# A two-layer hybrid attention decoder on one core: first four tiles side by side over pieces of weights and activations

## The chip, the cores and the metric

The kernel runs on one core of a Trainium2 chip. The metric is the device time of one execution in microseconds (us); lower is better. Inputs lie in the chip's memory at the start, the output there at the end.

## The reference, cut to what matters

Two layers on 272 tokens (16 learned ones and 256 of x) with 1024 channels, all in float32:

```
h    = rms_norm(r, norm_mix_pre[layer])
proj = h @ w_in[layer]          # q latent | kv latent | rope key | dq | dk | dv | gate_A | gate_B
out_a = causal_attention(...) @ w_o_mla      # from the latents
out_b = causal_diff_attention(...) @ w_o_diff
mix  = (sigmoid(g_a) * out_a + sigmoid(g_b) * out_b) @ w_out
r    = r + rms_norm(mix, norm_mix_post)
h    = rms_norm(r, norm_ffn_pre)
r    = r + rms_norm((silu(h @ w_gate) * (h @ w_up)) @ w_down, norm_ffn_post)
```

`rms_norm(x, gain)` is x / sqrt(mean(x*x) + 1e-6) * gain. The change touches the first norm of layer 0 and the first six column tiles of its `proj` (the latents and the rope key).

## The kernel before

**Layout.** Activations lie transposed: 128 channels on the partitions, 272 tokens in a row, 8 chunks of channels (`KC`). A tile is 128 columns of a weight matrix for all tokens, in one PSUM bank: 8 chunks k times three matmuls of 128x272. Three, because each float32 operand is split into a rounded part (`hi`, type fp32r) and a rest (`lo`): hi x hi, lo x hi and hi x lo are summed.

**Weights.** They are packed on the host into slots of 128 x 1024 values (512 KB), one for a tile of `proj`. SP (the sync engine) loads slot n into `w_raw[n % 4]`, and has to wait until VectorE has taken slot n - 4 apart (`lo_ready`, L285). ScalarE (ACT) rounds a slot into `w_hi` (`split`, L334 to L344), VectorE (DVE) subtracts into `w_lo` (`split`, L693 to L701); `w_hi` and `w_lo` are rings of 8.

**The norm.** The factor 1/sqrt(mean) belongs to a token, so it is applied when a tile is evacuated (`evac`, L715), not to the activations before. ScalarE multiplies the residual by the gain and rounds it (`first_hi`, L380), VectorE makes the rest (`lo_part`, L720). ScalarE also squares the residual (`square`, L346); GpSimd (POOL) adds up the squares of chunks 0 to 6 (`sum_squares`, L619), with two buffers for squares, so that a square waits for the add two before. TensorE (PE) sums over the partitions with 12 matmuls against ones (`norm_sums`, L1163), ScalarE takes the root (`root`), VectorE the reciprocal (`recip`), TensorE spreads it over the partitions by three transposes (`norm_spread`, L1194) and VectorE copies it out as `rstd_h` (`take`, L710). Only then can tile 0 be evacuated.

**Banks.** Tiles go round four banks (`t % BANKS`); a tile waits until the one four before it has been evacuated (`bank_free`, L1102). Bank 7 holds the norm's sums and its spread, bank 6 the throwaway matmuls of `keep_clock` (L1182).

**The order at the start.** SP issues, in this order: gains, x chunks 0-1, the first half of slots 0 and 1 together, x 2-3, x 4-5, the second half, x 6-7, the identity, slots 2, 3, 4, the rotary tables, slot 5, masks and lambdas (L291 to L305). ScalarE and VectorE work on slots 0 and 1 in quarters (`quarter_split`, L385 and L750). TensorE runs 50 throwaway matmuls (L1199), then tiles 0 and 1 side by side, chunk after chunk (`first_tiles`, L1123), tile 2, the norm's sums, tile 3 with the spread before its chunk 6, and tiles 4 and 5 (L1222). VectorE's order behind the spread: for each of the five latent tiles an evacuation, a weight split and a `lat_lo` (L810 to L822), with masks and lambda sums after the fourth; then the rotary factors, a split and tile 5 (L827 to L838); then the tiles of dq, dk and so on.

Of the kernel before, what the change touches and what calls it, by code (L numbers as in the profile page):

```python
# [23 lines left out]
P = 128  # L24
# [72 lines left out]

C_ID, C_MASK, C_MASKM, C_COSD, C_SIND, C_COSM, C_SINM = 0, 128, 256, 512, 784, 1056, 1328
# [49 lines left out]
def build_trunk(nc: bass.Bass, xT, weights, gains, lam_in, consts, gain_rows, out):  # L148
# [4 lines left out]
    with ctx:  # L153
# [3 lines left out]
        def place(at, tensors):  # L157
# [7 lines left out]
        (w_raw, w_hi, w_lo, r, hh, hl, y, rstd_h, rstd_q, acc, sq, rc_d, rs_d, rc_q, rs_q,  # L165
         cst, identb, maskb, gain, small, lat, tres), at = place(base, [
            ("w_raw", [P, RAW, SLOT], f32), ("w_hi", [P, RING, SLOT], f32r), ("w_lo", [P, RING, SLOT], f32r),
            ("resid", [P, KC, TOK], f32), ("h_hi", [P, KC, TOK], f32r), ("h_lo", [P, KC, TOK], f32r),
# [5 lines left out]
            ("gain", [P, DEPTH, GAINS], f32), ("small", [P, 96], f32), ("lat", [P, 2, TOK], f32),  # L174
            ("tres", [P, TOK], f32)])
        lat_tmp_at = at - 4 * 3 * TOK
        rstd_kv = tres
# [6 lines left out]
        k_t = nc.alloc_sbuf_tensor_at("k_t", [P, MLA_HEADS, TOK], f32, offset=base + 4 * (RAW + 2 * RING) * SLOT + 3 * 4 * KC * TOK)  # L184
# [15 lines left out]
        krope = dv_t[:, 0, :]  # L200
        dqk_at = att0 + 4 * MLA_HEADS * TOK
# [7 lines left out]
        (o_tok, o_sq), _ = place(base + 4 * (RAW + 2 * RING) * SLOT + 4 * KC * TOK, [("o_tok", [P, 2, D_MODEL], f32), ("o_sq", [P, 2, D_MODEL], f32)])  # L209
        assert _ <= base + 4 * (RAW + 2 * RING) * SLOT + 12 * KC * TOK  # L210
# [57 lines left out]

        def T0(l):

            return 0 if l < DEPTH - 1 else N_META
# [61 lines left out]
        def _(act):  # L333
            def split(n, i=None, per=0):  # L334
# [5 lines left out]
                act.wait_ge(raw_in[n % RAW], 16 * (n // RAW + (n % RAW >= 2)) + v)  # L340
# [34 lines left out]

            act.wait_ge(const_ready, 1)
            act.activation(idle_act, eps, ACT.Sqrt)
            act.wait_ge(gain_in, 16)

            def first_hi(*chunks):  # L380
                for c in chunks:
                    act.wait_ge(x_in[c // 2], 16)
                    act.activation(hh[:, c, :], r[:, c, :], ACT.Copy, scale=gain[:, 0, G_MIXPRE + c:G_MIXPRE + c + 1]).then_inc(h_hi, 1)

            def quarter_split(q):  # L385
# [21 lines left out]
            for n in range(3, AHEAD):  # L407
                split(n)
# [1182 lines left out]
```

## Time and profile before

| | |
|---|---|
| median of 3 runs | 835.7 us (835.64 to 836.18) |
| the profiled execution | 835.84 us, of which span 834.0 us |
| TensorE busy | 819.4 us (98%) |
| VectorE busy | 595.4 us (71%) |
| ScalarE busy | 451.9 us (54%) |
| GpSimd busy | 123.4 us (15%) |
| read from memory | 129.70 MB |

How to read it: the span is the time from the first to the last instruction, and the shares are of it. A share is a mean over stages with different limits, so the timeline of an engine and the table by stretches of time are read beside it. TensorE's matmuls are pipelined: the time from the start of one to the start of the next is its price, and is shorter than its own duration. The weight load that goes with each matmul overlaps the one before. The granted clock (PEclk) is 1.00 for 2.4 GHz and 0.50 for 1.2 GHz.

### The profile page before, as it was taken

The page shows a single profiled execution, that of the slowest core. Times are in us where ns is not written, and L with a number is a line of the kernel's source. Part 1 is how long each engine was busy: PE and PEld are TensorE (multiplying, and loading weights), DVE is VectorE, ACT ScalarE, POOL GpSimd, SP SyncE. Part 2 cuts the span into 40 slices and gives each one's busy share as a digit, 9 for nine tenths or more (in the row PEclk, how much of TensorE's full clock was granted, in tenths as well). Part 3 has the DMA queues.
Part 4 walks back from the last instruction along what each step waited for, and adds up shares of the span by engine and source line. Part 5 has one row for each costly group of instructions (what it writes and reads, how often), then busy time and mean ns, then how long its engine had stood idle before and what let it go on. Part 6 is the DMA issues. An engine that isn't in the chain of part 4 may idle for free.

```text
span 834.0 us, 17173 instructions
## 1 busy us (share of the span) xinstructions
PE 819.4 (98%) x6453; PEld 792.6 (95%) x6453; DVE 595.4 (71%) x1000; ACT 451.9 (54%) x749; POOL 123.4 (15%) x125
## 2 busy tenths in 40 slices
PE   8999999999999999999999999999999999999997
PEld 8998999999999999999999999899999999999885
DVE  4999586669597666666668995876787976766432
ACT  6755555475565444455556546554765654554431
POOL 2122000004331111101112220000053111111000
PEclk9999999999999999999999999999999999999999
DMA  8656422235526545445552555222363565565631
GB/s 280 224 189 205 148 77 102 76 103 181 173 88 217 180 172 177 131 139 185 178 199 86 200 195 185 95 101 99 108 224 103 182 219 182 177 194 172 207 104 50
DMA packets 38744, 131.55 MB, mean 158 GB/s; under 512 B 4384, under 2 KB 4768, under 8 KB 38688
## 3 DMA queue, kind: packets, MB, share of 16 engines
q1 hardware_dynamic: 38688, 130.77, 47.0%
q8 instruction: 39, 0.64, 0.3%
q14 instruction: 17, 0.14, 0.1%
HBM read 129.70 MB, written 1.05 MB: 157 GB/s over the span
## 4 chain that ended last, share of the span: by engine, by line
PE 84%; DVE 12%; issue 2%; ACT 1%; DMA 1%; SPq 0%; DVEq 0%; POOL 0%; POOLq 0%
PE bank L1110 21%; PE bank L1112 20%; PE bank L1111 20%; DVE w_lo L700 3%; PE bank L1140 3%; PE bank L1462 2%; PE bank L1463 2%; PE bank L1461 2%; PE bank L1335 2%; PE bank L1311 2%; PE bank L1159 2%; PE bank L1144 1%; DVE h_lo L722 1%; PE bank L1350 1%; DVE resid L737 1%
## 5 line engine op out<-in xcount | busy, mean ns | idle before, releaser
L700 DVE TENSOR_TENSOR w_lo<-w_raw,w_hi 128x1024 fp32r<-128x1024 f32 x250 | 336.0, 1346 | 39.2 <-ACT w_hi L344 37.1
L1110 PE MATMUL bank<-h_hi,w_hi 128*128 128x272 f32 (+1 forms) x1232 | 357.6, 290 | 2.1 <-DVE dv_t L718 0.9
L1112 PE MATMUL bank<-h_hi,w_lo 128*128 128x272 f32 (+1 forms) x1232 | 352.1, 286 | 0.0
L1111 PE MATMUL bank<-h_lo,w_hi 128*128 128x272 f32 (+1 forms) x1232 | 351.3, 285 | 0.0
L344 ACT ACTIVATE w_hi<-w_raw 128x1024 fp32r<-128x1024 f32 x250 | 262.6, 1054 | 127.7 <-PE bank L1112 54.7
L1110 PEld LDWEIGHTS bank<-h_hi,w_hi 128*128 128x128 f32 x1232 | 232.0, 188 | 4.2 <-issue 1.3
L1112 PEld LDWEIGHTS bank<-h_hi,w_lo 128*128 128x128 f32 x1232 | 231.9, 188 | 0.0
L1111 PEld LDWEIGHTS bank<-h_lo,w_hi 128*128 128x128 f32 x1232 | 231.6, 188 | 0.0
L624 POOL TENSOR_TENSOR acc<-acc,sq 128x272 f32<-128x272 f32 (+1 forms) x48 | 48.5, 1011 | 148.2 <-ACT sq L357 147.6
L669 POOL TENSOR_TENSOR pbuf<-sbuf,ubuf 128x272 f32<-128x272 f32 (+1 forms) x44 | 37.4, 850 | 210.2 <-DVE ubuf L1048 207.2
L1048 DVE TENSOR_TENSOR ubuf<-bank,rstd_h 128x272 f32<-128x272 f32 (+1 forms) x44 | 19.0, 431 | 48.1 <-PE bank L1112 48.0
L1110 PE MATMUL bank<-ff_hi,w_hi 128*128 128x272 f32 x176 | 50.7, 288 | 0.0
L1112 PE MATMUL bank<-ff_hi,w_lo 128*128 128x272 f32 x176 | 50.6, 288 | 0.0
L1111 PE MATMUL bank<-ff_lo,w_hi 128*128 128x272 f32 x176 | 50.6, 287 | 0.0
L573 ACT ACTIVATE sbuf<-gbuf 128x272 f32<-128x272 f32 (+1 forms) x44 | 18.7, 424 | 54.1 <-DVE gbuf L1048 54.1
L657 POOL TENSOR_TENSOR gates<-gates 128x272 f32<-128x272 f32 (+1 forms) x16 | 15.7, 1004 | 208.9 <-DVE gates L718 208.9
L473 ACT ACTIVATE e_t<-bank,small 128x272 f32<-128x272 f32 x64 | 27.0, 431 | 31.0 <-DVE small L912 31.0
L1140 PE MATMUL bank<-h_hi,w_hi 128*128 128x272 f32 (+1 forms) x144 | 38.6, 295 | 2.2 <-DVE w_lo L754 1.8
L1140 PE MATMUL bank<-h_hi,w_lo 128*128 128x272 f32 (+1 forms) x144 | 37.9, 289 | 0.0
L1462 PE MATMUL bank<-w_lo,ff_hi 128*128 128x512 f32 x88 | 34.7, 395 | 0.0
L1463 PE MATMUL bank<-w_hi,ff_lo 128*128 128x512 f32 x88 | 34.7, 394 | 0.0
L1461 PE MATMUL bank<-w_hi,ff_hi 128*128 128x512 f32 x88 | 34.6, 394 | 0.0
(209 smaller groups left out, 1250.6 us busy)
## 6 DMA issues: line engine op xcount, KB each, us to landing
w_raw<-weights SPq DMA_DIRECT2D x220, 512.0 KB, 4.0
w_raw<-weights SPq DMA_DIRECT2D x16, 384.0 KB, 3.0
w_raw<-weights SPq DMA_DIRECT2D x16, 320.0 KB, 2.8
resid<-x_t SPq DMA_DIRECT2D x4, 272.0 KB, 5.4
out_tokens<-o_tok SPq DMA_DIRECT2D x4, 256.0 KB, 2.0
cst<-consts SPq DMA_DIRECT2D x1, 544.0 KB, 4.9
gain_bc<-gain_rows SPq DMA_DIRECT2D x1, 512.0 KB, 6.7
y<-consts SPq DMA_DIRECT2D x1, 256.0 KB, 5.3
```

The source lines that it names most:

```text
L344: act.activation(w_hi[:, n % RING, :], w_raw[:, n % RAW, :], ACT.Copy).then_inc(hi_ready, 1)
L473: last = act.activation(e_t[:, e, a:b], ps[bank][:, a:b], ACT.Exp, bias=mx[u % 2][:, s + part:s + part + 1], scale=scale, accum_out=sm[u % ...
L624: pool.tensor_tensor(acc[:, K % 2, t0:], acc[:, K % 2, t0:], sq[:, plan.sq_place[K, c], t0:], ALU.add).then_inc(sq_added, 1)
L669: pool.tensor_tensor(pbuf[:, j % 2, t0:], sbuf_[:, j % 2, t0:], ubuf[:, j % 2, t0:], ALU.mult).then_inc(ff_prod, 1)
L700: dve.tensor_tensor(w_lo[:, n % RING, :], w_raw[:, n % RAW, :], w_hi[:, n % RING, :].bitcast(f32), ALU.subtract).then_inc(lo_ready, 1)
L1110: pe.matmul(dst, wh, hi, start=first, stop=False)
L1111: pe.matmul(dst, wh, lo, start=False, stop=False)
L1112: return pe.matmul(dst, wl, hi, start=False, stop=last)
L1140: pe.matmul(ps[t % BANKS][:, t0:TOK], w[:, n % RING, k * P:(k + 1) * P], src[k][0], start=k == 0 and q == 0, stop=False)
L1461: pe.matmul(dst, x_hi, wh, start=k == 0, stop=False)
L1462: pe.matmul(dst, x_hi, wl, start=False, stop=False)
L1463: return pe.matmul(dst, x_lo, wh, start=False, stop=k == FC - 1)
```

## The change

- The first four weight slots come in a tensor of their own, `first_weights`, packed by five pieces of chunks: (0), (1), (2, 3), (4, 5), (6, 7), each with those chunks' columns of all four tiles. They land in a buffer of their own, `w_first`, that lies where later q and k are kept. Gains and x come in one tensor: 80 columns of gains, then x.
- SP issues the five weight pieces, and the x of the last two pieces ahead of their weights. ScalarE issues the x of the first three pieces from its own queue, before anything else.
- Slots 4 to 7 go into the four raw buffers without a wait.
- ScalarE does, for each piece: its activations, their squares, and the split of the piece for four tiles. VectorE does the lo parts and the split of the same piece.
- TensorE runs tiles 0 to 3 side by side, piece by piece: hi x hi of the piece's chunks, then lo x hi, then hi x lo. Tiles 4 and 5 take banks 4 and 5, so that no tile waits for a bank before tile 6. The norm's sums stand at chunk 0 of tile 4, the spread at its chunk 5.
- 34 throwaway matmuls at the start instead of 50.
- On VectorE one split moves from the second latent tile to the third, where two now stand.

```diff
+GAIN_COLS = 80
+FIRST = 4
+PIECES = [(0, 1), (1, 2), (2, 4), (4, 6), (6, 8)]
+X_BY_ACT = 3
...
+            ("x_sb", [P, GAIN_COLS + KC * TOK], f32), ("h_hi", [P, KC, TOK], f32r), ("h_lo", [P, KC, TOK], f32r),
+        r = x_sb[:, GAIN_COLS:].rearrange("p (k t) -> p k t", k=KC)
+        gain = x_sb[:, 0:DEPTH * GAINS].rearrange("p (l g) -> p l g", l=DEPTH)
+        (w_first,), _ = place(att0, [("w_first", [P, FIRST * SLOT], f32)])
...
+        def piece_of(w, a, b):
+            return w[:, FIRST * P * a:FIRST * P * b].rearrange("p (s c) -> p s c", s=FIRST)
+        def x_cols(q):
+            a, b = PIECES[q]
+            return slice(GAIN_COLS + a * TOK if q else 0, GAIN_COLS + b * TOK)
+        def bank_of(t):
+            return t if t < FIRST + 2 else t % BANKS
...
-                if n >= RAW:
+                if n >= FIRST + RAW:
...
-            xc = xT.rearrange("p (k t) -> p k t", k=KC)
-            sp.dma_start(gain[:, :, :], gains.rearrange("p (l g) -> p l g", l=DEPTH)).then_inc(gain_in, 16)
-            two = weights[0:2 * P, :].rearrange("(s p) c -> p s c", s=2)
-            for q in range(4):
-                sp.dma_start(r[:, 2 * q:2 * q + 2, :], xc[:, 2 * q:2 * q + 2, :]).then_inc(x_in[q], 16)
-                if q in (0, 2):
-                    at = q * SLOT // 4
-                    sp.dma_start(w_raw[:, 0:2, at:at + SLOT // 2], two[:, :, at:at + SLOT // 2]).then_inc(half_in[q // 2], 16)
+            for q, (a, b) in enumerate(PIECES):
+                ws = slice(FIRST * P * a, FIRST * P * b)
+                if q >= X_BY_ACT:
+                    sp.dma_start(x_sb[:, x_cols(q)], xT[:, x_cols(q)]).then_inc(x_in[q], 16)
+                sp.dma_start(w_first[:, ws], first_weights[:, ws]).then_inc(piece_in[q], 16)
             sp.dma_start(cst[:, 0:P], consts[:, 0:P]).then_inc(id_in, 16)
-            load(2, SLOT)
-            load(3, SLOT)
             load(4, SLOT)
+            load(5, SLOT)
             sp.dma_start(cst[:, P:], consts[:, 512:C_ALL]).then_inc(tables_in, 16)
-            load(5, SLOT)
+            load(6, SLOT)
+            load(7, SLOT)
             sp.dma_start(stage, consts[:, P:512 + P].rearrange("p (a b) -> p a b", a=2)[:, :, 0:256]).then_inc(mask_in, 16)
             sp.dma_start(lam_raw, lam_in).then_inc(mask_in, 16)
-            first = 6
+            first = FIRST + RAW
...
+            for q in range(X_BY_ACT):
+                act.dma_start(x_sb[:, x_cols(q)], xT[:, x_cols(q)]).then_inc(x_in[q], 16)
...
+            def first_hi(q):
+                act.wait_ge(x_in[q], 16)
+                for c in range(*PIECES[q]):
                     act.activation(hh[:, c, :], r[:, c, :], ACT.Copy, scale=gain[:, 0, G_MIXPRE + c:G_MIXPRE + c + 1]).then_inc(h_hi, 1)
+            def piece_split(q):
+                act.wait_ge(piece_in[q], 16)
+                a, b = PIECES[q]
+                ins = act.activation(w_hi[:, 0:FIRST, a * P:b * P], piece_of(w_first, a, b), ACT.Copy)
+                if b == KC:
+                    ins.then_inc(hi_ready, FIRST)
+                else:
+                    ins.then_inc(piece_hi, 1)
-            first_hi(0, 1)
-            quarter_split(0)
-            quarter_split(1)
-            first_hi(2, 3)
-            first_squares(0, 1)
-            first_hi(4, 5)
-            quarter_split(2)
-            quarter_split(3)
-            first_hi(6, 7)
-            first_squares(2)
-            split(2)
-            first_squares(3, 4, 5, 6, 7)
-            for n in range(3, AHEAD):
-                split(n)
+            for q in range(len(PIECES)):
+                first_hi(q)
+                first_squares(*range(*PIECES[q]))
+                piece_split(q)
+            split(FIRST)
+            split(FIRST + 1)
+            split(FIRST + 2)
...
-                if l == 0:
-                    split(AHEAD)
...
-            for c in range(KC):
-                lo_part(0, c, G_MIXPRE, 0, 0)
-                if c in (1, 5):
-                    quarter_split(c // 2)
-                    quarter_split(c // 2 + 1)
-            split(2)
-            split(3)
-            split(4)
-            split(5)
+            dve.wait_ge(x_in[0], 16)
+
+            def piece_split(q):
+
+                a, b = PIECES[q]
+                if b == KC:
+                    dve.wait_ge(hi_ready, FIRST)
+                else:
+                    dve.wait_ge(piece_hi, q + 1)
+                ins = dve.tensor_tensor(w_lo[:, 0:FIRST, a * P:b * P], piece_of(w_first, a, b), w_hi[:, 0:FIRST, a * P:b * P].bitcast(f32), ALU.subtract)
+                if b == KC:
+                    ins.then_inc(lo_ready, FIRST)
+                else:
+                    ins.then_inc(piece_lo, 1)
+
+            for q, (a, b) in enumerate(PIECES):
+                dve.wait_ge(x_in[q], 16)
+                for c in range(a, b):
+                    lo_part(0, c, G_MIXPRE, 0, 0)
+                piece_split(q)
+            split(FIRST)
+            split(FIRST + 1)
...
-                    if i or not l:
-                        split(S("lat") + i + AHEAD)
+                    if l or i != 1:
+                        if l == 0 and i == 2:
+                            split(S("lat") + 1 + AHEAD)
+                        if i or not l:
...
-                if t >= BANKS:
+                if t >= FIRST + 2:
...
+            def start_tiles(src):
+                for q, (a, b) in enumerate(PIECES):
+                    for k in range(a, b):
+                        pe.wait_ge(h_hi, k + 1)
+                        if b == KC:
+                            pe.wait_ge(hi_ready, FIRST)
+                        else:
+                            pe.wait_ge(piece_hi, q + 1)
+                        for t in range(FIRST):
+                            pe.matmul(ps[t][:, :TOK], w_hi[:, t, k * P:(k + 1) * P], src[k][0], start=k == 0, stop=False)
+                    for k in range(a, b):
+                        pe.wait_ge(h_lo, k + 1)
+                        for t in range(FIRST):
+                            pe.matmul(ps[t][:, :TOK], w_hi[:, t, k * P:(k + 1) * P], src[k][1], start=False, stop=False)
+                    if b == KC:
+                        slot_ready(FIRST - 1)
+                    else:
+                        pe.wait_ge(piece_lo, q + 1)
+                    for k in range(a, b):
+                        for t in range(FIRST):
+                            mm = pe.matmul(ps[t][:, :TOK], w_lo[:, t, k * P:(k + 1) * P], src[k][0], start=False, stop=k == KC - 1)
+                            if k == KC - 1:
+                                mm.then_inc(pe_done, 1)
...
-            keep_clock(50)
+            keep_clock(34)
...
-                    first_tiles([(TL("lat") + q, S("lat") + q, late, t0) for q in range(2)], (h_hi, h_lo, 0),
-                                {0: lambda: pe.wait_ge(quarter_lo, 1), 2: lambda: pe.wait_ge(quarter_lo, 2),
-                                 4: lambda: pe.wait_ge(quarter_lo, 3), 6: lambda: slot_ready(1)})
-                    slot_ready(S("lat") + 2)
-                    tile(TL("lat") + 2, S("lat") + 2, 0, P, late, t0)
-                    norm_sums(K0 + PRE_MIX, 7, 0)
-                    pe.wait_ge(id_in, 16)
-                    slot_ready(S("lat") + 3)
-                    tile(TL("lat") + 3, S("lat") + 3, 0, P, full, 0, inside={6: lambda: norm_spread(K0 + PRE_MIX, 7, 0)})
+                    start_tiles(full)
...
-                    tile(TL("lat") + i, S("lat") + i, 0, P if i < 5 else HW, full, 0)
+                    def first_spread():
+                        pe.wait_ge(id_in, 16)
+                        norm_spread(PRE_MIX, 7, 0)
+                    tile(TL("lat") + i, S("lat") + i, 0, P if i < 5 else HW, full, 0,
+                         inside={0: lambda: norm_sums(PRE_MIX, 7, 0), 5: first_spread} if (l, i) == (0, 4) else None)
...
+    x_t = np.concatenate([gains, np.zeros((P, GAIN_COLS - DEPTH * GAINS), np.float32), x_t], axis=1)
...
+    first = packed[0:FIRST * P].reshape(FIRST, P, SLOT)
+    first = np.concatenate([first[:, :, a * P:b * P].transpose(1, 0, 2).reshape(P, -1) for a, b in PIECES], axis=1)
```

## Rows read from the trace of the kernel before

**Rows 1.** The page: busy us; two groups with busy, mean ns | idle.
```profile
PE 819.4 (98%) x6453; PEld 792.6 (95%) x6453; DVE 595.4 (71%) x1000; ACT 451.9 (54%) x749; POOL 123.4 (15%) x125
...
L700 DVE TENSOR_TENSOR w_lo<-w_raw,w_hi 128x1024 fp32r<-128x1024 f32 x250 | 336.0, 1346 | 39.2 <-ACT w_hi L344 37.1
...
L624 POOL TENSOR_TENSOR acc<-acc,sq 128x272 f32<-128x272 f32 (+1 forms) x48 | 48.5, 1011 | 148.2 <-ACT sq L357 147.6
```

**Rows 2.** TensorE's timeline: start, length, operation, count [idle before <-releaser].
```profile
1.06 5.18 PE L1185 MATMUL bank<-identb 128*128 128x128 bf16 x50 [1.06 <-DVE identb L747]
8.08 0.39 PE L1140 MATMUL bank<-h_hi,w_hi 128*128 128x272 f32 x1 [1.84 <-DVE w_lo L754]
...
10.10 0.43 PE L1140 MATMUL bank<-h_hi,w_hi 128*128 128x272 f32 x1
10.33 0.43 PE L1140 MATMUL bank<-h_hi,w_lo 128*128 128x272 f32 x1
...
15.73 0.28 PE L1110 MATMUL bank<-h_hi,w_hi 128*128 128x272 f32 x1
...
18.76 0.72 PE L1159 MATMUL bank<-small,acc 128*128 128x1 f32 x6
...
20.01 0.37 PE L1110 MATMUL bank<-h_hi,w_hi 128*128 128x272 f32 x1
...
22.48 0.54 PE L1178 MATMUL bank<-cst,small 128*128 128x128 f32 x3
...
40.39 0.36 PE L1110 MATMUL bank<-h_hi,w_hi 128*128 128x272 f32 x1 [0.94 <-DVE dv_t L718]
...
78.13 0.39 PE L1110 MATMUL bank<-lat_hi,w_hi 128*128 128x272 f32 x1 [0.55 <-DVE dv_t L718]
```

**Rows 3.** Stretches: length, busy by engine, granted clock, DMA share, GB/s.
```profile
9.20:12.60 3.40, 3.40 (x18) 3.40 (x17) 3.12 (x7) 3.40 (x9) 0.98 (x2) 0.50 0.89 354
```

**Rows 4.** The same view for VectorE alone.
```profile
23.05:81.70 58.65, 57.00 (x101) 1.00 0.61 203
```

**Rows 5.** VectorE's timeline.
```profile
23.06 0.44 DVE L713 COPY rstd_h<-bank 128x272 f32<-128x272 f32 x1 [0.64 <-PE bank L1178]
23.53 0.44 DVE L718 TENSOR_TENSOR lat<-bank,rstd_h 128x272 f32<-128x272 f32 x1
...
25.85 0.50 DVE L821 SCALAR_TENSOR_TENSOR lat_lo<-lat,gain,lat_hi 128x272 fp32r<-128x272 f32 x1 [0.74 <-ACT lat_hi L425]
...
28.62 1.45 DVE L700 TENSOR_TENSOR w_lo<-w_raw,w_hi 128x1024 fp32r<-128x1024 f32 x1
29.99 1.02 DVE L821 SCALAR_TENSOR_TENSOR lat_lo<-lat,gain,lat_hi 128x272 fp32r<-128x272 f32 x1
```

**Rows 6.** ScalarE's timeline.
```profile
0.74 1.28 ACT L377 ACT_TABLE_LOAD   x1 [0.74 <-PEq L1585]
...
8.56 0.41 ACT L357 ACTIVATE acc<-resid 128x272 f32<-128x272 f32 x1
...
9.20 0.92 ACT L383 ACTIVATE h_hi<-resid,gain 128x272 fp32r<-128x272 f32 x2
10.03 1.14 ACT L389 ACTIVATE w_hi<-w_raw 128x512 fp32r<-128x512 f32 x2
11.06 0.92 ACT L383 ACTIVATE h_hi<-resid,gain 128x272 fp32r<-128x272 f32 x2
```

**Rows 7.** SP's timeline; transfers, us to landing; a stretch as in rows 3.
```profile
1.19 0.42 SPq L294 DMA_DIRECT2D resid<-x_t  x1
1.66 0.43 SPq L297 DMA_DIRECT2D w_raw<-weights  x1
...
resid<-x_t SPq DMA_DIRECT2D x1, 272.0 KB, 3.5
w_raw<-weights SPq DMA_DIRECT2D x1, 512.0 KB, 5.0
...
3.00:5.00 2.00, 2.00 (x22) 2.00 (x21) 0.00 (x0) 0.22 (x1) 0.00 (x0) 1.00 0.92 315
```

More of the change, by code:

```diff
@@ L145, in __init__, with build_trunk @@
                     s += CHUNKS[k]
-def build_trunk(nc: bass.Bass, xT, weights, gains, lam_in, consts, gain_rows, out):
+def build_trunk(nc: bass.Bass, xT, first_weights, weights, lam_in, consts, gain_rows, out):
     f32, f32r, bf16 = mybir.dt.float32, mybir.dt.float32r, mybir.dt.bfloat16
@@ L163, in place @@
             return made, at
-        (w_raw, w_hi, w_lo, r, hh, hl, y, rstd_h, rstd_q, acc, sq, rc_d, rs_d, rc_q, rs_q,
-         cst, identb, maskb, gain, small, lat, tres), at = place(base, [
+        (w_raw, w_hi, w_lo, x_sb, hh, hl, y, rstd_h, rstd_q, acc, sq, rc_d, rs_d, rc_q, rs_q,
+         cst, identb, maskb, small, lat, tres), at = place(base, [
             ("w_raw", [P, RAW, SLOT], f32), ("w_hi", [P, RING, SLOT], f32r), ("w_lo", [P, RING, SLOT], f32r),
-            ("resid", [P, KC, TOK], f32), ("h_hi", [P, KC, TOK], f32r), ("h_lo", [P, KC, TOK], f32r),
+            ("x_sb", [P, GAIN_COLS + KC * TOK], f32), ("h_hi", [P, KC, TOK], f32r), ("h_lo", [P, KC, TOK], f32r),
             ("y", [P, KC, TOK], f32),
@@ L173, in build_trunk @@
             ("cst", [P, C_ALL - 512 + 128], f32), ("identb", [P, P], bf16), ("maskb", [P, P], bf16),
-            ("gain", [P, DEPTH, GAINS], f32), ("small", [P, 96], f32), ("lat", [P, 2, TOK], f32),
+            ("small", [P, 96], f32), ("lat", [P, 2, TOK], f32),
             ("tres", [P, TOK], f32)])
         lat_tmp_at = at - 4 * 3 * TOK
+        r = x_sb[:, GAIN_COLS:].rearrange("p (k t) -> p k t", k=KC)
+        gain = x_sb[:, 0:DEPTH * GAINS].rearrange("p (l g) -> p l g", l=DEPTH)
         rstd_kv = tres
@@ L373, in boundary @@
                     square(K, c, r[:, c, t0:], t0)
+            for q in range(X_BY_ACT):
+                act.dma_start(x_sb[:, x_cols(q)], xT[:, x_cols(q)]).then_inc(x_in[q], 16)
             act.wait_ge(const_ready, 1)
             act.activation(idle_act, eps, ACT.Sqrt)
[L378 to L382, printed above, removed]
+            def first_hi(q):
+                act.wait_ge(x_in[q], 16)
+                for c in range(*PIECES[q]):
                     act.activation(hh[:, c, :], r[:, c, :], ACT.Copy, scale=gain[:, 0, G_MIXPRE + c:G_MIXPRE + c + 1]).then_inc(h_hi, 1)
-            def quarter_split(q):
-                act.wait_ge(half_in[q // 2], 16)
-                cols = slice(q * SLOT // 4, (q + 1) * SLOT // 4)
-                act.activation(w_hi[:, 0:2, cols], w_raw[:, 0:2, cols], ACT.Copy).then_inc(hi_ready if q == 3 else quarter_hi, 2 if q == 3 else 1)
+            def piece_split(q):
[6 more added lines that the diff above has]
+                    ins.then_inc(piece_hi, 1)
             def first_squares(*chunks):
@@ L717, in evac @@
                 dve.wait_ge(pe_done, plan.tile_done[t])
-                dve.tensor_tensor(dst, ps[t % BANKS][rows, t0:TOK], factor, ALU.mult).then_inc(tile_free, 1)
+                dve.tensor_tensor(dst, ps[bank_of(t)][rows, t0:TOK], factor, ALU.mult).then_inc(tile_free, 1)
             def lo_part(b, c, g, l, t0):
@@ L1581 @@
     gain_rows = np.broadcast_to(A(norm_ffn_post)[DEPTH - 1][None, :], (P, D_MODEL))
-    arrays = {"x_t": x_t, "weights": packed, "gains": gains, "lam": lam, "consts": constants(), "gain_rows": gain_rows}
+    first = packed[0:FIRST * P].reshape(FIRST, P, SLOT)
+    first = np.concatenate([first[:, :, a * P:b * P].transpose(1, 0, 2).reshape(P, -1) for a, b in PIECES], axis=1)
+    arrays = {"x_t": x_t, "first_weights": first, "weights": packed, "lam": lam, "consts": constants(), "gain_rows": gain_rows}
     arrays = {k: np.ascontiguousarray(v) for k, v in arrays.items()}
```

27 lines of the change are left out of this document (11 added, 16 removed).

## The prediction, made before the changed kernel had run

> **What bounds the kernel now.** First the page's busy shares: TensorE is busy for 98% of the span [rows 1], so a change can only give time where TensorE idles, runs slowly or does more than it must. Next its own timeline [rows 2]. Fifty warm-up matmuls run from 1.06 to 6.24 us; the first real matmul starts at 8.08, after 1.84 us of idle. From there to 78 us there are few gaps: 0.94 us before 40.39 and 0.55 us before 78.13 are the ones shown, both released by a VectorE evacuation. After 78.13 VectorE is no longer what holds TensorE in this layer. The pitch of a matmul is read from two neighbours: tile 2 has 24 of them from 15.73 to 18.76, 0.126 us each, while at 10.10 and 10.33 the pitch is 0.23. The table by stretches says why: from 9.20 to 12.60 the granted clock is 0.50, which is 1.2 GHz, and the pitch at 15.73 is that of 2.4 GHz again; what TensorE did before that fall was its idle time up to 8.08 [rows 2, 3]. The 48 matmuls of tiles 0 and 1 took 7.65 us (8.08 to 15.73) where 0.126 each gives 6.05, so the low clock cost 1.6 us.
>
> The third view decides the case. From 23.05 to 81.70 VectorE is busy 57.00 of 58.65 us [rows 4], and the only idle time that I find behind its start at 23.06 is 0.74 us at 25.85 [rows 5]. That chain starts when rstd_h is copied out (23.06), runs through evacuations, weight splits and rotary factors, and TensorE, with a ring of four banks, waits for it. The waits at 40.39 and 78.13 are for it. So for this stage the end is set by when the evacuation of tile 0 can start (23.53) and by how long VectorE then needs, not by how early TensorE finished its first tiles. I reason with that start, and call it E.
>
> **Part 1, the start.** Before, x piece 0 is issued at 1.19 and lands 3.5 us later, at 4.7; the first weights, issued at 1.66, land at 6.7 [rows 7]. They were 0.84 MB together with the gains. After, piece 0 is 0.18 MB of x with gains on ACT's queue and 0.26 MB of weights on SP's, both issued at about 0.75. Against x piece 0 of before (0.32 MB with the gains) that is 0.12 MB more, 0.4 us at the 315 GB/s of 3 to 5 us, and the issue is 0.44 us earlier: weights at about 4.7, x at about 4.4. ScalarE's issues are three at SP's 0.42 us each; they push its table load, 0.74 to 2.02, to about 2.1 to 3.4 [rows 6, 7]: hidden behind the landing at 4.4. If an issue on ACT took far longer (1 us), the table would end at 5.1 and all below be 0.7 us late.
>
> ScalarE then works in series. From row to row: two activations 0.83, two squares 0.64, a 512-column split half of 1.03 [rows 6]. Per 128 rows of the model that is 0.42 + 0.32 + 0.52 = 1.25 us, against 12 matmuls at 0.126 = 1.5 us on TensorE. First matmul: 4.4 + 0.5 + 0.4 + 0.6 = 5.95 (from 8.08). The split of piece 2 (512 KB, for k = 2, 3) needs pieces 0 to 2, 1.67 MB: the first 0.84 MB landed at 6.66, the rest at 315 to 354 GB/s [rows 3, 7] takes 2.3 to 2.6 us, less 0.44: 8.5 to 8.8, I take 8.6. ScalarE by its own series is there at about 8.5. Split 1.05: k = 2 is ready at 9.7. TensorE has done k = 0, 1 at 5.95 + 3.0 = 8.95, and stalls 0.75. Pieces 3 and 4 are then ready at intervals of 2.5 us against 3.0 of TensorE, so 72 matmuls follow without a gap: 9.7 + 9.05 = 18.75.
>
> The Trainium skill speaks against a gain from the second queue here (DMA: Bandwidth & Descriptors, section "Issuing engines are not separate DMA queues": transfers from either issuer share the same engines, and only issue time is saved). This trace has no transfer from ACT, so it doesn't show it; by the rule the sum stands as written, and if instead the queues were independent the weights of piece 0 would land some 0.4 us sooner, and ScalarE, waiting for x, would still set 5.95.
>
> **Part 2, from there to E.** Before, the twelve norm-sum matmuls (18.76 to 20.01, 1.25 us) ran behind tile 2, and the spread at 22.48 came with six matmuls of tile 3 left. After, they stand at k = 0 of tile 4 and the spread at k = 5: 18.75 + 1.25 + 15 matmuls 1.9 + a handover of 0.1 + the 1.05 us from spread to evacuation (22.48 to 23.53) [rows 2, 5] = 23.05. So of 2.1 us won at the first matmul, 0.75 goes to the stall and 2.65 to the 21 matmuls that now stand ahead of the spread (96 + 15 where 90 were), while the low clock (1.6 us before) is not in this sum: by these differences E would move by 0.1, by the absolute sum by 0.5, since before had some 0.4 us of small gaps ahead of the spread. I take 0.5.
>
> The clock has to be put back in. Warm-up of 34 ends at about 1.06 + 34 x 0.104 = 4.6, idle is 1.35 us instead of 1.84, plus the stall. Nothing shows that this leaves the clock alone: bounds 0 and 1.6 us (the same fall as before). The first 0.75 us of a fall ahead of 9.7 would vanish in the stall. I take 0.3.
>
> **Part 3, behind E.** The VectorE chain from 23.53 to the evacuation of tile 5, which lets TensorE go on at 40.39, is 16.9 us with 0.74 idle [rows 2, 5]. Its instructions stay; one split moves from the second latent tile to the third. The 0.74 (a late raw weight for ScalarE) goes, since slots 4 to 7 are loaded without waiting for a free buffer. In its place the second lat_lo, no longer behind a split, must wait for ScalarE's split, activation and square: about 0.5. 16.9 - 0.74 + 0.5 is 16.6, so -0.3. Bounds: -1.2 (both go, and one of the two lat_lo that took 1.02 instead of 0.50 runs free) and +0.5. TensorE has tiles 4 to 8 done by about 18.75 + 1.75 + 15.1 = 35.6 and waits for the bank of tile 9 until E + 16.6, 39.6, so six banks and the early end of the first tiles buy nothing beyond E; the gap before 40.39 grows instead from 0.94 to about 4 us.
>
> Squares directly behind activations, the merged gain transfer and the shorter warm-up change nothing else: squares are in the series above, and GpSimd's six adds now run beside VectorE's lo parts. Rows show what an overlap can cost: the lat_lo at 29.99 took 1.02 where the one at 25.85 took 0.50, and the split before it 1.45 against a mean of 1.35 [rows 1, 5]. A pair of chunks needs two lo parts and one 1024-column split, 1.0 + 1.35 = 2.35 us, against 3.0 of TensorE, which wants the split's result last: one such loss of 0.5 for each pair is covered. The Trainium skill (SBUF — State Buffer, "Who interferes with whom") has a VectorE operation with two SBUF inputs and a GpSimd operation that reads SBUF block each other completely; the 1.02 agrees.
>
> **Sum.** -0.5 (E) - 0.3 (chain) + 0.3 (clock) = -0.5 us on the profiled execution, 835.84 (span 834.0 and 1.84 around it). The median is 835.7, the highest 836.18, so the profiled one is 0.14 over the median: 835.3 us.
>
> **Rivals.**
> *A, no change (42%), as above: 835.3.* For it: VectorE saturated behind E. Against: nothing but the sizes.
> *B, faster (27%).* x lands as soon as the table load allows (3.9), and so does everything in ScalarE's series (-0.5), the clock doesn't fall (-0.3), the chain gains the whole 1.2 (-0.9): 835.3 - 1.7 = 833.6. The real opposite would be that VectorE is elastic and TensorE's earlier end counts; the 57.00 of 58.65 speaks against it.
> *C, the clock falls as before, or the shared port decides (16%).* The fall costs 1.3 more than I took: 836.6. If each of the six adds held VectorE for its whole mean of 1.0 us [rows 1], a pair of chunks would cost it 2.35 + 2.0 = 4.35 against TensorE's 3.0; over the last two pairs that is 2.7 late, of which about 1 lies in the time that TensorE has before it wants the result: 1.7, so 837.0. Both lie inside 0.2%. That is what the rule of the Trainium skill on the shared port, named above, would make of it.
> *D, slower (15%).* Clock again, but longer: the start now has gaps (1.35 us, then the stall, then whatever piece comes late), and the half clock lasts twice as long as before, 6.8 us. About 30 matmuls at 0.1 more, 3.0 us, of which 0.3 is in the sum: 838.0. It decides once the low stretch reaches past some 5 us; against it stands that 1.84 us of idle brought only 3.4 us.
> *That the change doesn't do what it says:* x on ACT's queue lands no sooner than on SP's; then 5.95 becomes 6.5 and the result 835.9, inside A.
>
> **How the numbers follow.** What a measurement here can tell is about 0.2%, 1.7 us: faster means under 834.0, slower over 837.4. B gives 27% and A's edge 1%: 28% faster. A's rest and C: 57%. D: 15%. The range: below, B's 833.6 with a little for more of the chain, 833.4; above, C's 837.0 and the lower half of D, 837.8.
>
> **What would show it.** First real matmul at 5.6 to 6.3 us; a stall of 0.5 to 1 us after 24 matmuls; the end of the first four tiles near 18.8; tile 0 evacuated from about 23 us, and hardly sooner than before; VectorE still without idle time behind it; TensorE's wait before tile 9 grown to 3 to 4 us; the wait for dv_t near 78 still there. I am wrong if the evacuation of tile 0 starts more than 1.5 us from 23.05, if the low clock lasts beyond 5 us, or if VectorE turns out idle behind E.

## The result, and the profile after

The changed kernel takes 836.83 us in the median of 20 runs, the kernel before 835.81 us beside it: ratio 1.0015, 95% interval 1.0009 to 1.0021. It is 1.0 us slower, where 0.5 us faster was forecast (835.3). The change is inside the 0.2% that I called no change, and the sign is wrong. One of the 20 executions, at a mean granted clock of 0.752, took 987.16 us and is left out of the ratio.

The execution that was profiled first took 838.91 us, 2 us over its median. A second profile of the same kernel took 836.53, and is the one to compare with. First TensorE's timeline of the first profile (start, length, operation, count, idle before it and what ended it):

```profile
1.06 3.81 PE L1229 MATMUL bank<-identb 128*128 128x128 bf16 x34 [1.06 <-DVE identb L759]
6.09 0.74 PE L1178 MATMUL bank<-h_hi,w_hi 128*128 128x272 f32 x4 [1.22 <-ACT w_hi L406]
...
11.17 1.25 PE L1178 MATMUL bank<-h_hi,w_hi 128*128 128x272 f32 x8 [1.81 <-ACT w_hi L406]
...
29.97 0.36 PE L1129 MATMUL bank<-h_hi,w_hi 128*128 128x272 f32 x1 [0.32 <-DVE lat L730]
33.81 0.36 PE L1129 MATMUL bank<-h_hi,w_hi 128*128 128x272 f32 x1 [0.58 <-DVE lat L730]
42.70 0.36 PE L1129 MATMUL bank<-h_hi,w_hi 128*128 128x272 f32 x1 [2.40 <-DVE dv_t L730]
```

The first real matmul came at 6.09, 2.0 us sooner than before [rows 2]. But the stall ahead of piece 2 is 1.81 us, and the wait ahead of dq's last tile has grown from 0.94 to 2.40. ScalarE's timeline says what TensorE stalled for, and the transfers of piece 2 (weights, then x, both issued at about 1.66) what ScalarE waited for:

```profile
4.59 0.52 ACT L400 ACTIVATE h_hi<-x_sb 128x272 fp32r<-128x272 f32 x1 [0.94 <-DMA x_sb<-x_t]
...
6.86 0.62 ACT L406 ACTIVATE w_hi<-w_first 128x512 fp32r<-128x512 f32 x1
8.51 0.94 ACT L400 ACTIVATE h_hi<-x_sb 128x272 fp32r<-128x272 f32 x2 [1.03 <-DMA x_sb<-x_t]
9.35 0.73 ACT L373 ACTIVATE sq<-x_sb 128x272 f32<-128x272 f32 x2
9.99 1.04 ACT L406 ACTIVATE w_hi<-w_first 128x1024 fp32r<-128x1024 f32 x1
```

```profile
w_first<-first_weights SPq DMA_DIRECT2D x1, 512.0 KB, 6.4
x_sb<-x_t ACTq DMA_DIRECT2D x1, 272.0 KB, 6.8
```

Piece 2's x landed at about 8.5, behind its weights (8.1), though it is half their size and has only 0.3 MB ahead of it on its queue. Then activation, squares and split stand in a row, 8.51 to 11.0.

VectorE's timeline of the same profile. The row at 26.04 answers the 23.53 of before [rows 5]:

```profile
23.54 0.18 DVE L720 RECIPROCAL small<-small 128x3 f32<-128x3 f32 x1 [3.15 <-ACT small L381]
25.57 0.44 DVE L725 COPY rstd_h<-bank 128x272 f32<-128x272 f32 x1 [1.85 <-PE bank L1222]
26.04 0.44 DVE L730 TENSOR_TENSOR lat<-bank,rstd_h 128x272 f32<-128x272 f32 x1
...
28.97 0.50 DVE L840 SCALAR_TENSOR_TENSOR lat_lo<-lat,x_sb,lat_hi 128x272 fp32r<-128x272 f32 x1 [0.59 <-ACT lat_hi L437]
...
43.10 0.01 DVE L857 LOAD_MASK_SELECT b_t<-b_t  x1 [0.54 <-DVE dv_t L730]
...
53.05 0.33 DVE L720 RECIPROCAL small<-small 128x3 f32<-128x3 f32 x2 [0.65 <-ACT small L381]
```

VectorE was idle 1.85 us, for the most part while TensorE finished the five chunks of tile 4 ahead of the spread. The table by stretches (its bounds and length, busy by engine, then the granted clock, the DMA share and GB/s in the last three columns) shows why this execution was slower than the median. The clock was down behind the stall, and again behind the 2.40 us wait:

```profile
12.00:15.50 3.50, 3.50 (x19) 3.50 (x18) 3.50 (x4) 3.50 (x8) 2.64 (x3) 0.56 1.03 421
...
43.00:46.50 3.50, 3.50 (x18) 3.50 (x17) 3.19 (x12) 0.94 (x1) 1.71 (x2) 0.52 0.40 151
```

### The profile page after: what moved, and what is told of

Same layout as the page of the kernel before. It is cut to its first block, busy times and chain, and to the rows that moved or that the text cites. A ratio compares the mean times of both kernels' runs of the same rounds, so it can differ in the third digit from the quotient of the medians.

```text
span 837.1 us, 17151 instructions
## 1 busy us (share of the span) xinstructions
PE 819.5 (98%) x6437; PEld 792.9 (95%) x6437; DVE 596.6 (71%) x999; ACT 452.1 (54%) x748; POOL 123.4 (15%) x125
## 3 DMA queue, kind: packets, MB, share of 16 engines
HBM read 129.70 MB, written 1.05 MB: 156 GB/s over the span
## 4 chain that ended last, share of the span: by engine, by line
PE 81%; DVE 14%; issue 2%; ACT 1%; DMA 1%; ACTq 0%; DVEq 0%; POOL 0%; SPq 0%; POOLq 0%
PE bank L1129 20%; PE bank L1131 20%; PE bank L1130 19%; DVE w_lo L712 4%; PE bank L1504 2%; PE bank L1505 2%; PE bank L1503 2%; PE bank L1159 2%; PE bank L1377 2%; PE bank L1353 2%; PE bank L1203 1%; DVE h_lo L734 1%; PE bank L1392 1%; PE bank L1163 1%; DVE x_sb L749 1%
## 5 line engine op out<-in xcount | busy, mean ns | idle before, releaser
L1129 PE MATMUL bank<-h_hi,w_hi 128*128 128x272 f32 (+2 forms) x1216 | 353.7, 291 | 4.1 <-DVE dv_t L730 2.4
L1131 PE MATMUL bank<-h_hi,w_lo 128*128 128x272 f32 (+2 forms) x1216 | 348.2, 286 | 0.0
L1130 PE MATMUL bank<-h_lo,w_hi 128*128 128x272 f32 (+2 forms) x1216 | 347.5, 286 | 0.0
L1129 PEld LDWEIGHTS bank<-h_hi,w_hi 128*128 128x128 f32 (+1 forms) x1216 | 229.8, 189 | 6.4 <-DVE w_lo L712 2.6
L1131 PEld LDWEIGHTS bank<-h_hi,w_lo 128*128 128x128 f32 (+1 forms) x1216 | 229.6, 189 | 0.0
L1130 PEld LDWEIGHTS bank<-h_lo,w_hi 128*128 128x128 f32 (+1 forms) x1216 | 229.3, 189 | 0.0
L1159 PE MATMUL bank<-h_hi,w_hi 128*128 128x256 f32 (+1 forms) x128 | 33.4, 289 | 0.4
L1129 PEld LDWEIGHTS bank<-ff_hi,w_hi 128*128 128x128 f32 x176 | 33.1, 188 | 0.0
```

The lines of the kernel that those rows point to most:

```text
L1129: pe.matmul(dst, wh, hi, start=first, stop=False)
L1130: pe.matmul(dst, wh, lo, start=False, stop=False)
L1131: return pe.matmul(dst, wl, hi, start=False, stop=last)
L1159: pe.matmul(ps[t % BANKS][:, t0:TOK], w[:, n % RING, k * P:(k + 1) * P], src[k][0], start=k == 0 and q == 0, stop=False)
```

## The experiments

"E" is again the start of tile 0's evacuation on VectorE. Medians are of 10 or 11 runs each; the kernel before stood at 835.68, 835.71 and 835.76 in the three groups (32 or 33 runs each). Each edit is made to the changed kernel, but for the last. The 95% interval of each ratio to the kernel before is about 0.1% to either side, 0.7 to 0.8 us, so a difference of 0.2 to 0.4 us between two of these medians says little alone; E and the waits in the profiles say more. "The first" below is the median of the first experiment, 836.62. The theory under test: the time is E plus a constant, since VectorE is saturated behind E. Its rival: every TensorE instruction of the first 80 us counts.

**The changed kernel again.**

> The changed kernel itself, for a second profile and as the yardstick of this group. Its first profiled execution was 838.9 us, over 2 us above its median of 836.8, with the clock at half speed from 12.3 to 15.6 us (behind a 1.81 us stall for piece 2) and again from 43.1 to 46.5 us (behind a 2.40 us wait for tile 5's bank). If these falls are a matter of chance, this median is 836.8 again and the profile may lack one of them, with tile 0's evacuation then at 24.5 instead of 26.0 us. If they come every time, the profile shows both and the span is near 837.

Median 836.62. The same kernel's falls of the clock come at different times. In this profile, the first one lies from 7 to 10.4 us, over the matmuls of pieces 0 and 1 and where the stall had been, so TensorE shows no stall ahead of piece 2 at all, and E is 24.23:

```profile
7.00:10.40 3.40, 3.40 (x18) 3.40 (x17) 2.06 (x4) 2.61 (x6) 1.67 (x2) 0.52 1.04 416
41.60:45.00 3.40, 3.40 (x17) 3.40 (x17) 3.20 (x11) 1.06 (x1) 1.71 (x2) 0.55 0.37 133
```

```profile
24.23 0.44 DVE L730 TENSOR_TENSOR lat<-bank,rstd_h 128x272 f32<-128x272 f32 x1
```

```profile
40.89 0.36 PE L1129 MATMUL bank<-h_hi,w_hi 128*128 128x272 f32 x1 [2.40 <-DVE dv_t L730]
```

The span is 834.8. Span less E is 810.6, before it was 834.0 - 23.53 = 810.5: 0.7 of the 0.8 us between the spans is E.

**Throwaway matmuls in the stall.**

> The changed kernel with 46 throwaway matmuls at the start instead of 34 and 26 more ahead of the matmuls of piece 2, where TensorE stalled 1.81 us. If the stall makes the clock fall at 12.3, the fall goes, the evacuation of tile 0 comes about 1.4 us earlier in a profile that had it, and the median gains 0.5 to 1.5 us against the changed kernel. If the clock has nothing to do with it, the median stays within 0.3 us.

```
+                    if q == 2:
+                        keep_clock(26)
...
-            keep_clock(34)
+            keep_clock(46)
```

Median 836.84, 0.2 over the first. In the profile the clock is full from 3 to 18 us and E is 24.54, so keeping the clock up buys nothing in the median. Half clock over pieces 0 and 1 is free while piece 2 is late, as the profile above shows. Of the five profiled executions with the changed kernel's start (the first profile and those of the first, third, seventh and eighth experiment) only the first paid for a fall. That most others don't pay either would account for the missing gain, but no trace shows it.

**Throwaway matmuls in the late gap.**

> The changed kernel with 26 throwaway matmuls (about 1.5 us) on TensorE ahead of dq's last tile, where it waited 2.40 us for VectorE. VectorE theory (what counts is when tile 0 is evacuated and VectorE's work behind it): costs nothing, and gains up to 1 us where it keeps the clock from falling at 43. TensorE theory (every TensorE instruction in the first 80 us counts): 1.5 us slower than the changed kernel.

```
+                        if l == 0 and st == "dq" and i == 3:
+                            keep_clock(26)
```

Median 837.26, 0.64 over the first: neither 0 nor 1.5. The wait ahead of dq's last tile shrank from 2.40 to 0.94 and that tile began at E + 16.67, as without the fillers, and the low clock behind it was gone. So the 1.5 us on TensorE weren't paid there, and the second fall of the clock had not cost anything either. E was 24.48 here, 0.25 later than in the first experiment's profile; some 0.35 us of the span appeared only behind 431 us, and stay unexplained.

**Sums and spread earlier.**

> The changed kernel with the norm's 12 sum matmuls ahead of the last eight hi x lo matmuls of the first four tiles, and the spread ahead of tile 4's chunk 0 instead of chunk 5. TensorE does exactly the same work. VectorE theory: the spread comes 15 matmuls earlier, tile 0's evacuation 1.9 us, and the time falls by 1.5 to 1.9 us to about 835.0. TensorE theory: nothing changes (within 0.3 us).

```
                     if b == KC:
+                        norm_sums(PRE_MIX, 7, 0)
                         slot_ready(FIRST - 1)
...
-  inside={0: lambda: norm_sums(PRE_MIX, 7, 0), 5: first_spread}
+  inside={0: first_spread}
```

Median 834.90, 1.72 under the first, with the same instructions on every engine. E is 22.93 and the span 833.4, 810.5 apart. This experiment decides: TensorE's amount of work is untouched, and the time follows the place of 12 + 3 small matmuls. From the first matmul of k = 2 to E it is 11.46 us where it is 13.34 in the first experiment's profile: 1.88 less, the 15 matmuls at 0.126. E itself moved by 1.3 only, since piece 2 was even later in this profile (11.47):

```profile
11.47 1.24 PE L1178 MATMUL bank<-h_hi,w_hi 128*128 128x272 f32 x8 [1.95 <-ACT w_hi L406]
...
39.60 0.36 PE L1129 MATMUL bank<-h_hi,w_hi 128*128 128x272 f32 x1 [2.07 <-DVE dv_t L730]
```

**Split ahead of the squares.**

> The changed kernel with each piece's weight split ahead of its squares on ScalarE instead of behind them. In the profiles so far piece 2's x landed at 8.2 to 8.8 us and its weights before that, so the two squares (0.64 us) stood between the activation and the split that TensorE waited for. VectorE theory with the late x as the cause: the stall ahead of piece 2 shrinks by 0.6 us, tile 0 is evacuated 0.6 us sooner (at about 23.8) and the median is 0.6 below the changed kernel's 836.6. Rival (the stall is hidden, or GpSimd's adds become late): within 0.2 us.

```
-                first_squares(*range(*PIECES[q]))
                 piece_split(q)
+                first_squares(*range(*PIECES[q]))
```

Median 836.23, 0.39 under the first: the direction is as expected and the size two thirds. In the profile x of piece 2 landed at 8.1 and ScalarE's split of piece 2 ended at 9.96, yet E is 24.11, just 0.12 sooner than in the first experiment. TensorE was late itself this time:

```profile
6.08 1.25 PE L1178 MATMUL bank<-h_hi,w_hi 128*128 128x272 f32 x4 [1.21 <-ACT w_hi L406]
...
10.85 1.16 PE L1178 MATMUL bank<-h_hi,w_hi 128*128 128x272 f32 x8
```

The granted clock reads 1.00 here, but the rows show half speed: the four matmuls at 6.08 take 1.25 us where the first profile has 0.74, and the 24 of pieces 0 and 1 take 4.77 where 24 at 0.126 are 3.0. Where TensorE waits for that split, k = 2 starts 0.14 us behind its end in the other profiles, which would be 10.1 here; it started at 10.85 and without a wait. So half speed over pieces 0 and 1 is free only while piece 2 is late, and here it cost some 0.7 us.

**All x by SP.**

> The changed kernel with all five x transfers on SP's queue, each ahead of its weights, and none on ScalarE's. If x of piece 2 lands late (8.2 to 8.8 us) because SP's later transfers share the DMA engines with ScalarE's queue, it lands by 8 us here, ahead of its weights, the stall shrinks by 0.5 to 1 us, and the median falls to 835.8 to 836.2. If the second queue is what brings x early, x lands later, the first real matmul comes 0.5 us later than 6.2 and the median is 0.3 to 1 us above the changed kernel's.

```
-X_BY_ACT = 3
+X_BY_ACT = 0
```

Median 838.01, from 836.46 to 838.86. Both halves of what I expected failed in part. x of piece 0 landed 2.3 us after its issue instead of 3.8 to 4.1, and the first real matmul came at 5.09, a full 1.1 us sooner. But the weights of piece 2, whose issue had moved from 1.66 to 3.07 behind the x transfers, landed at 9.7 instead of 8.1. ScalarE had to wait for them, and the stall stayed (1.80 us):

```profile
7.82 0.94 ACT L400 ACTIVATE h_hi<-x_sb 128x272 fp32r<-128x272 f32 x2 [1.23 <-DMA x_sb<-x_t]
8.66 0.73 ACT L373 ACTIVATE sq<-x_sb 128x272 f32<-128x272 f32 x2
9.72 1.06 ACT L406 ACTIVATE w_hi<-w_first 128x1024 fp32r<-128x1024 f32 x1 [0.33 <-DMA w_first<-first_weights]
```

The profiled execution (836.46) is the fastest of them, with E at 24.27. What the slower ones had isn't seen: a longer pause between a sooner start and the same k = 2 could bring the clock down where it isn't covered, as in the very first profile, but no trace shows it.

**Tile 5 in its old bank.**

> The changed kernel with tile 5 back in bank 1, so that it waits for tile 1's evacuation (five banks instead of six at the start). VectorE theory: TensorE waits about 1 to 2 us earlier, but has 2.4 us to spare ahead of dq's last tile, so nothing moves (within 0.3 us). TensorE theory: 1 to 2 us slower.

```
-            return t if t < FIRST + 2 else t % BANKS
+            return t if t < FIRST + 1 else t % BANKS
...
-                if t >= FIRST + 2:
+                if t >= FIRST + 1:
```

Median 836.83, 0.2 over the first, E 24.20, span 834.8 as in it. TensorE waits 1.86 us ahead of tile 5, and begins dq's last tile at the same distance from E:

```profile
26.68 0.34 PE L1129 MATMUL bank<-h_hi,w_hi 128*96 128x272 f32 x1 [1.86 <-DVE lat L730]
40.88 0.36 PE L1129 MATMUL bank<-h_hi,w_hi 128*128 128x272 f32 x1 [1.90 <-DVE dv_t L730]
```

So the sixth bank is worth nothing that can be measured here.

**One more operation on VectorE.**

> The changed kernel with one more VectorE operation on 128x1024 values (about 1.1 to 1.2 us, result unused) right behind the evacuation of tile 0. VectorE theory: the whole 1.1 us is paid, median 837.7. TensorE theory: TensorE has its first six tiles in six banks and is not held, within 0.3 us of 836.6.

```
                     evac(TL("lat") + i, ...)
+                    if l == 0 and i == 0:
+                        dve.tensor_tensor(q_t[:, 0:4, 0:256], r[:, 2:6, 0:256], r[:, 2:6, 0:256], ALU.subtract)
```

Median 837.55, 0.9 over the first. E is 24.64 and dq's last tile begins at 42.42, E + 17.78: 1.12 more than the 16.66 of the others, the price of the operation. Span less E is 811.3, so 0.7 of it is left at the end of the kernel; behind dq's last tile VectorE's wait of 0.54 us that the first experiment's profile has at 41.29 is gone, which can make up the rest. The TensorE theory allowed 0.3 us in all, the VectorE theory the whole 1.1. The median is near the second; the profile says that 0.7 of the 1.1 was paid.

**Both edits that moved E.**

> The changed kernel with both single edits that moved tile 0's evacuation: the sums ahead of the last eight matmuls with the spread at tile 4's start (-1.7 us alone) and each split ahead of its squares (-0.4 us alone). VectorE theory: they add up, evacuation of tile 0 at about 22.6 us, median 834.5, faster than the kernel before (835.7) by 1.2.

It is both edits shown above. Median 834.23, ratio to before 0.9982 (0.9973 to 0.9991). E 21.90, span 832.4: again 810.5 apart. Against the sums and the spread alone (834.90) the split ahead of the squares gains 0.67 here, the whole of what I expected of it. The changed kernel's own start, put in another order, beats the kernel before.

**The spread inside the first four tiles.**

> The changed kernel with splits ahead of squares and, in the last piece of the first four tiles, the sums ahead of the lo x hi matmuls and the spread ahead of the hi x lo matmuls, so that rstd_h is there when the four tiles end. VectorE theory: evacuation of tile 0 at about 22.1 us, median 834.0 to 834.2. Rival: the reciprocal stands behind two splits on VectorE and TensorE now waits for it; then about as the sums-and-split version, 834.5.

```
+                    if b == KC:
+                        norm_sums(PRE_MIX, 7, 0)
                     for k in range(a, b):
                         pe.wait_ge(h_lo, k + 1)
...
                     if b == KC:
+                        pe.wait_ge(id_in, 16)
+                        norm_spread(PRE_MIX, 7, 0)
                         slot_ready(FIRST - 1)
```

Median 834.17, ratio 0.9981 (0.9972 to 0.9990): the same as the one above within what is measured. The profile has E at 21.59, 0.3 sooner, but its k = 2 came at 10.15 against 10.45, and from k = 2 to E it is 11.44 us against 11.45: the new place of the spread gained nothing. As the rival said, the reciprocal stood behind two splits, and TensorE waited 0.58 for it. TensorE's rows, then VectorE's:

```profile
16.75 0.67 PE L1178 MATMUL bank<-h_hi,w_hi 128*128 128x272 f32 x4
17.25 0.72 PE L1207 MATMUL bank<-small,acc 128*128 128x1 f32 x6
17.84 0.81 PE L1207 MATMUL bank<-small,sq 128*128 128x1 f32 x6
...
20.34 0.51 PE L1226 MATMUL bank<-cst,small 128*128 128x128 f32 x3 [0.58 <-DVE small L720]
```

```profile
17.76 2.35 DVE L712 TENSOR_TENSOR w_lo<-w_raw,w_hi 128x1024 fp32r<-128x1024 f32 x2
20.03 0.16 DVE L720 RECIPROCAL small<-small 128x3 f32<-128x3 f32 x1
20.89 0.44 DVE L725 COPY rstd_h<-bank 128x272 f32<-128x272 f32 x1 [0.70 <-PE bank L1226]
21.59 0.44 DVE L730 TENSOR_TENSOR lat<-bank,rstd_h 128x272 f32<-128x272 f32 x1 [0.26 <-PE bank L1193]
```

**x of piece 2 by SP.**

> The changed kernel with the x of piece 2 issued by SP, ahead of piece 2's weights, and only the first two by ScalarE. If the late x of piece 2 is due to the sharing of the DMA engines between two queues, it lands 0.5 us sooner (7.7 to 8.1 us), the stall ahead of piece 2 shrinks and the median falls by 0.3 to 0.6 from 836.6. If not, it stays within 0.2 us.

```
-X_BY_ACT = 3
+X_BY_ACT = 2
```

Median 836.20, 0.42 under the first. x of piece 2, issued at 1.66 as in the changed kernel, lands 5.4 us later, at about 7.1; ScalarE no longer waits for it, the stall ahead of piece 2 is down to 0.66, and E is 23.72, the soonest of the kernels that leave sums and spread in place. The two transfers of piece 2, then TensorE's row:

```profile
x_sb<-x_t SPq DMA_DIRECT2D x1, 272.0 KB, 5.4
w_first<-first_weights SPq DMA_DIRECT2D x1, 512.0 KB, 6.5
```

```profile
10.38 1.23 PE L1178 MATMUL bank<-h_hi,w_hi 128*128 128x272 f32 x8 [0.66 <-ACT w_hi L406]
```

With the same issue time it landed 1.0 to 1.7 us sooner than from ScalarE's queue (8.1 to 8.8 in ten profiles). So the late x is the work of its place on that queue, beside SP's. The weights of piece 2 are issued behind it now, at 2.13, and land at 8.6.

**The kernel before, with its spread earlier.**

> The kernel before, not the changed one, with the norm's spread ahead of tile 3's chunk 2 instead of 6, the root and the reciprocal ahead of slot 5's split, and that split behind tile 0's evacuation. VectorE theory: tile 0 is evacuated 1.7 us sooner (about 21.8 us), VectorE's work behind it grows by one split (1.15 us), so 0.5 us faster than before, 835.2. TensorE theory: no change.

```
-            for n in range(3, AHEAD):
+            for n in range(3, AHEAD - 1):
...
                 root(K0 + PRE_MIX, 7, D_MODEL, 0)
                 if l == 0:
+                    split(AHEAD - 1)
...
             split(4)
-            split(5)
             recip(PRE_MIX, 0)
...
+                    if i == 0 and not l:
+                        split(AHEAD - 1)
...
-  inside={6: lambda: norm_spread(K0 + PRE_MIX, 7, 0)}
+  inside={2: lambda: norm_spread(K0 + PRE_MIX, 7, 0)}
```

Median 835.64, the same as before (ratio 1.0000, 0.9991 to 1.0009). E went from 23.53 to 22.45, only 1.1 instead of 1.7 sooner: the reciprocal still stood behind two splits and came at 20.81 (22.25 before), and the spread behind it ran at half clock. One split of 1.15 moved behind E, so -1.1 + 1.15 = 0 would explain the median. The profile doesn't settle it. TensorE ran at half clock from 20.4 to 23.8 us, and the 0.94 us that it had to spare ahead of dq's last tile are gone. It began that tile at 40.05 (counted off in its matmuls), E + 17.60, and its first wait for VectorE behind the spread is this one:

```profile
64.56 0.39 PE L1112 MATMUL bank<-lat_hi,w_hi 128*128 128x272 f32 x1 [0.72 <-DVE gates L719]
```

The span is 833.4, 0.6 us shorter than before, in an execution of 835.14 that is 0.5 under its median. So an edit that moves work across E gained nothing in the median, and which engine took the gain back is open.

## Why the prediction was wrong

What bounds the stage was right. In twelve of the fourteen profiles dq's last tile begins 16.6 to 16.9 us behind E; the other two are the one with an operation added (17.78) and the last one (17.60), where a split was moved and TensorE's clock was down behind the spread. It holds to the end of the kernel too: E and span are 23.53 and 834.0 before, then 24.23 and 834.8, 22.93 and 833.4, 24.11 and 834.7, 21.90 and 832.4, 21.59 and 832.0, and ten profiles have them 810.4 to 810.6 apart. (The four others: 811.1 in the very first profile, 810.9 with late fillers, 811.3 with the operation added, 811.0 in the last.) So the gain or loss is E's, and the step that failed is the one that placed E. E was to be 23.05, 0.5 sooner than before; it is 24.20 to 24.64 in the four later profiles with the changed kernel's start, and 26.04 in the first. More than 1.5 us off was the prediction's own sign of being wrong; the first and one of the four (24.64) are.

**Part 1, "ScalarE by its own series is there at about 8.5".** The first real matmul was about right (5.95 forecast, 6.09 to 6.38 measured). The split of piece 2 was to be done at 9.7; it was done at 11.0 to 11.3 (k = 2 at 11.17, 11.12, 11.29 and 11.47 in four profiles). The sum had checked when the weights land (8.6, measured 8.1) and taken for granted that x was there. x landed at 8.1 to 8.8, and activation 0.84, squares 0.64 and split 1.0 came behind it. So k = 2 came 1.4 to 1.8 us late, and ScalarE's wait for this x, put at nothing, is the larger share: 1.03 us in the first profile, 0.7 to 1.2 in the others with this start. The rest is ScalarE's own series, which the sum had too short: it began at 4.59 instead of 4.4, waited 0.16 for the x of piece 1 and spent 0.61 on each small split instead of 0.52. With piece 2's x from SP ScalarE had no wait for it, and k = 2 still came at 10.38, 0.7 late. In the traces a small transfer on ScalarE's queue was as late as the big ones that ran beside it on SP's; from SP's queue, with the same issue time, it landed at 7.1. The rule of the Trainium skill that I quoted (DMA: Bandwidth & Descriptors, "Issuing engines are not separate DMA queues") agrees with this; I had applied it to piece 0 only.

**Part 2.** From k = 2 on the sum was right: 11.12 + 9.05 + 1.25 + 1.9 + 0.1 + 1.05 = 24.47, and the profile with k = 2 at 11.12 and full clock has E at 24.48. The 21 matmuls ahead of the spread are the other large term. They were in the sum at 2.65 us, rightly. The fourth experiment put 15 matmuls behind the spread instead of ahead of it, and the last eight of the first four tiles between the sums and the spread; the median fell by 1.7 us. One slip in the working did no harm: by the differences, 2.1 - 0.75 - 2.65 + 1.6, E would move by 0.3 and not by 0.1; the 0.5 that I took is from the absolute sum.

**The clock.** I took 0.3. In the median it is about 0: E is 24.20 to 24.64 in five profiles (the first, second, third, seventh and eighth experiment), with and without a fall. Where the fall lies ahead of k = 2 the stall hides it, as long as piece 2 is late; where it lies behind, as in the first profile, it costs 1.5 us of E (14.87 us from k = 2 to E against 13.34), and that execution was 2 us slower.

**Part 3, -0.3 for the chain.** Up to dq's last tile it was -0.2 (16.66 against 16.86), with the exchange as forecast: 0.74 us of idle gone, 0.59 at the second lat_lo in its place. But a wait of VectorE on its own evacuation of tile 5 took 0.54 where before there were some 0.1 us between the two instructions, and the end of the kernel shows none of the -0.3: 810.6 against 810.5. I have no reason for the 0.54. It wasn't there in the profile with one more VectorE operation. The wait ahead of dq's last tile, forecast at 3 to 4 us, is 2.40: in the same profiles TensorE waits 0.32 and 0.58 us for the evacuations of latent tiles on its way there, for which the sum had nothing. That cost no time.

The sum with what was measured: E from 23.53 to between 24.2 and 24.64, chain 0: +0.7 to +1.1, against +1.0 in the medians. None of the priced rivals was this one. The nearest was the last, x on ACT's queue landing no sooner than on SP's. It was so (piece 0 at 3.1 from SP against 4.6 to 4.9, piece 2 at 7.1 against 8.1 to 8.8), but it was thought through for the first matmul only, at 0.6 us. The shared port (C) was felt but didn't decide. In VectorE's timeline of the first profile, the split at 11.06 and the pairs of lo parts at 12.58 and 15.57 ran beside GpSimd's adds and took longer than the pair at 9.13, nearly all of it alone, and the split at 14.43. Beside that split it was GpSimd's add that got longer (the last row: 1.60 us, where one add took 0.83 at 7.03):

```profile
9.13 0.92 DVE L734 SCALAR_TENSOR_TENSOR h_lo<-x_sb,h_hi 128x272 fp32r<-128x272 f32 x2 [0.72 <-ACT h_hi L400]
11.06 1.60 DVE L769 TENSOR_TENSOR w_lo<-w_first,w_hi 128x1024 fp32r<-128x1024 f32 x1 [1.01 <-ACT w_hi L406]
12.58 1.93 DVE L734 SCALAR_TENSOR_TENSOR h_lo<-x_sb,h_hi 128x272 fp32r<-128x272 f32 x2
14.43 1.21 DVE L769 TENSOR_TENSOR w_lo<-w_first,w_hi 128x1024 fp32r<-128x1024 f32 x1
15.57 1.42 DVE L734 SCALAR_TENSOR_TENSOR h_lo<-x_sb,h_hi 128x272 fp32r<-128x272 f32 x2
...
14.67 1.60 POOL L636 TENSOR_TENSOR acc<-acc,sq 128x272 f32<-128x272 f32 x1 [0.46 <-ACT sq L373]
```

Yet TensorE had no wait for VectorE in the first four tiles: both of its waits there end with ScalarE. D did not come: no low stretch that the clock column or the matmul rows show was longer than 3.8 us.

## What to carry to other kernels

Find the engine that is saturated behind the start and the event that lets it begin, and judge every edit by when that event comes; here the first matmul came 2 us sooner and the kernel took 1 us longer. When a stage needs two transfers, work out the landing of both, and count against each all bytes in flight on every queue, not those on its own. Small serial work that releases the saturated engine (sums, root, reciprocal, spread) goes ahead of bulk matmuls as soon as its inputs exist: here that alone was worth 1.7 us.

## What the hardware showed that I had not expected

- Two transfers issued together at 1.66 us from two queues, 272 KB and 512 KB, landed 6.8 and 6.4 us later: the smaller one last. With every transfer on SP's queue, the first transfer (176 KB) landed in 2.3 us instead of 3.8 to 4.1, and the first real matmul came 1.1 us sooner.
- Two stretches of half clock of 3.4 us in one execution of 836.53 us cost nothing that the median shows; the same kernel with the first stretch 5 us later took 838.91.
- The granted clock can read 1.00 while the matmuls run at half speed: in the profiles of the fifth and seventh experiment the four matmuls of the first chunk took 1.25 and 1.24 us instead of 0.74. The start times of the matmuls are the surer sign.
